# Transposes on TensorE: four 64x64 products with a 64x64 identity in place of one 128x128 transpose

## What is computed

```python
# HGRN2, for each of 8 heads: k * exp(...) and v with positions on the partitions
u_chunk = jnp.einsum('bhnlk,bhnlv->bhnkv', k * jnp.exp(cum_last - cum), v)
# gated MLP, for each of 8 groups: v with positions on the partitions
sv = jnp.einsum('gts,bnsgc->bntgc', w, v) + b_s.T[None, None, :, :, None]
# retention, for each of 4 pairs of heads and 2 layers: keys and values
kv = jnp.einsum('bnjhd,bnjhe,hj->nbhde', kc, vc, zeta)
# attention, for each of 8 heads and 2 layers: the probabilities
o = jnp.einsum('bnhgqs,bnshd->bnqhgd', p.astype(v.dtype), vb)
```

## Time and profile before

| what | value |
|---|---|
| runs, median (lowest to highest) | 2947.54 us (2946.81 to 2949.56) |
| profiled execution, from its first to its last instruction (span) | 2947.4 us |
| TensorE products busy | 2914.6 us, 99% |
| GpSimd busy | 1474.3 us, 50% |
| VectorE busy | 1289.6 us, 44% |
| ScalarE busy | 1093.7 us, 37% |
| mean granted clock of TensorE | 0.998 of full speed |

### The profile page before, as it was taken

The page is one execution under the profiler, slowest core; times in us unless marked ns, Lnnn a source line. Parts: engine busy times, 40 slices in busy tenths (PEclk is TensorE's granted clock), DMA queues, the critical chain, the costliest instruction groups (busy, mean ns, idle before and its releaser), DMA issues.

```text
span 2947.4 us, 52217 instructions
## 1 busy us (share of the span) xinstructions
PE 2914.6 (99%) x20726; PEld 2340.7 (79%) x20726; DVE 1289.6 (44%) x1814; ACT 1093.7 (37%) x1536; POOL 1474.3 (50%) x1824
## 2 busy tenths in 40 slices
PE   9999999999999999999999999999999999999999
PEld 5887778878888777777778888887777777888887
DVE  5827742381111658433657222225944365732210
ACT  4455653352222443224553322224322445432322
POOL 4643345545555556224337555665622433755555
PEclk9999999999999999999999999999999999999999
DMA  7731132313233233226343222333322633432233
GB/s 265 277 102 51 51 99 87 99 52 107 94 99 106 86 109 125 70 75 222 101 160 116 95 94 99 103 105 117 119 71 81 212 110 129 142 99 94 98 101 127
DMA packets 104761, 335.21 MB, mean 114 GB/s; under 512 B 10608, under 2 KB 11024, under 8 KB 103824
## 3 DMA queue, kind: packets, MB, share of 16 engines
q1 hardware_dynamic: 77648, 277.06, 28.6%
q10 hardware_dynamic: 26944, 55.67, 5.1%
HBM read 303.84 MB, written 28.84 MB: 113 GB/s over the span
## 4 chain that ended last, share of the span: by engine, by line
PE 79%; issue 8%; POOL 6%; DVE 4%; ACT 1%; DVEq 1%; DMA 1%; ACTq 0%; POOLq 0%; SPq 0%
PE psum L405 68%; POOL w_lo L376 6%; PE psum L795 5%; DVEq L1720 1%; DMA arena<-scratch 1%; DVE XL L1723 1%; PE psum L1046 0%; PE psum L1026 0%; PE psum L534 0%; PE psum L1040 0%; PE psum L544 0%; PE psum L1062 0%; DVE arena L1741 0%; PE psum L734 0%; PE psum L982 0%
## 5 line engine op out<-in xcount | busy, mean ns | idle before, releaser
L376 POOL TENSOR_TENSOR w_lo<-w_raw,w_hi 128x256 fp32r<-128x256 f32 x1820 | 1474.1, 841 | 1468.4 <-ACT w_hi L1098 1320.1
L405 PE MATMUL psum<-XH,w_hi 128*128 128x512 f32 x2592 | 1047.1, 404 | 10.7 <-DVE arena L1969 3.5
L405 PE MATMUL psum<-XL,w_hi 128*128 128x512 f32 x2592 | 1012.5, 391 | 0.0
L405 PE MATMUL psum<-XH,w_lo 128*128 128x512 f32 x2592 | 1012.4, 391 | 0.0
L1098 ACT ACTIVATE w_hi<-w_raw 128x1024 fp32r<-128x1024 f32 x436 | 460.4, 1056 | 685.0 <-PE psum L405 580.6
L405 PEld LDWEIGHTS psum<-XH,w_hi 128*128 128x128 f32 x2592 | 487.4, 188 | 135.9 <-issue 19.4
L405 PEld LDWEIGHTS psum<-XL,w_hi 128*128 128x128 f32 x2592 | 487.5, 188 | 104.2
L405 PEld LDWEIGHTS psum<-XH,w_lo 128*128 128x128 f32 x2592 | 487.9, 188 | 101.2 <-issue 7.7
L405 PE MATMUL psum<-HH,w_hi 128*128 128x512 f32 x976 | 383.0, 392 | 3.4 <-DVE arena L2354 3.4
L405 PE MATMUL psum<-HL,w_hi 128*128 128x512 f32 x976 | 379.9, 389 | 0.0
L405 PE MATMUL psum<-HH,w_lo 128*128 128x512 f32 x976 | 379.8, 389 | 0.0
(11 more groups left out here) (345 smaller groups left out, 2368.0 us busy)
## 6 DMA issues: line engine op xcount, KB each, us to landing
w_raw<-in_fills SPq DMA_DIRECT2D x456, 512.0 KB, 3.3
scratch<-arena ACTq DMA_DIRECT2D x86, 256.0 KB, 2.1
arena<-in_fills SPq DMA_DIRECT2D x32, 512.0 KB, 4.2
arena<-scratch ACTq DMA_DIRECT2D x10, 1024.0 KB, 7.7
arena<-in_w_ada SPq DMA_DIRECT2D x4, 2048.0 KB, 19.6
H<-scratch ACTq DMA_DIRECT2D x4, 2048.0 KB, 11.5
scratch<-H SPq DMA_DIRECT2D x2, 2048.0 KB, 8.1
arena<-scratch SPq DMA_DIRECT2D x32, 128.0 KB, 3.8
```

The costliest lines, as they stand in the source:

```text
L376: ins = nc.gpsimd.tensor_tensor(w_lo[:, to:to + FILL // 4], w_raw[:, of:of + FILL // 4], w_hi[:, to:to + FILL // 4].bitcast(F32), ALU.subt ...
L405: ins = mm(out_ap, wt[:, w:w + 128], xt[:, x0:x0 + T], start=first and k == 0 and o == 0, stop=last and k == n - 1 and o == 2)
```

## The change

A new helper, `quarter_transposes`, issues four products of 64x64 for each block of 128x128: for each half `j` of the block's columns and each half `i` of its rows, the quarter of the source is the weight and `eye64` is the moving operand. The upper rows go into one bank, the lower rows into a second one. The helper replaces `transposes` at HGRN, gated MLP and retention and the loop of transposes of the attention probabilities. ScalarE's copies keep their size and read the two banks alternately in runs of 64 columns (`turned`, `blocks_of`). In the gated MLP the transposes now need banks 4 and 5, and the products that follow go to banks 6 and 7 in place of 5 and 7.

```diff
+        def turned(b, b1, at, n):
+            both = psum[:, 512 * b:512 * (2 * b1 - b)].rearrange("p (i x) -> p i x", i=2)[:, :, at:at + 64 * n]
+            return both.rearrange("p i (k c) -> p k i c", c=64)
+
+        def blocks_of(ap):
+            return ap.rearrange("p (k i c) -> p k i c", i=2, c=64)
...
+            def quarter_transposes(b, b1, at, src, n=4):
+                for k in range(n):
+                    for j in range(2):
+                        for i, bb in enumerate((b, b1)):
+                            r = slice(64 * i, 64 * i + 64)
+                            ins = mm(bank(bb, 64, at + 64 * k)[64 * j:64 * j + 64], src(k)[r, 64 * j:64 * j + 64], C("eye64", 64)[r],
+                                     start=True, stop=True)
+                return ins
...
-                transposes(4, lambda k: hg("kdec", 128, 128 * k))
-                transposes(5, lambda k: A(60, 128, h * T + 128 * k)).then_inc(sem("hg_tr"), 1)
+                quarter_transposes(4, 5, 0, lambda k: hg("kdec", 128, 128 * k))
+                quarter_transposes(4, 5, 256, lambda k: A(60, 128, h * T + 128 * k)).then_inc(sem("hg_tr"), 1)
...
-                transposes(4, lambda k: A(60, 128, g * T + 128 * k)).then_inc(sem("gm_tr"), 1)
+                quarter_transposes(4, 5, 0, lambda k: A(60, 128, g * T + 128 * k)).then_inc(sem("gm_tr"), 1)
...
-                    ins = mm(bank(5 + 2 * (g % 2), 128, 128 * b), A(42, 128, 128 * b), A(32, 128, 128 * g), start=True, stop=True)
+                    ins = mm(bank(6 + g % 2, 128, 128 * b), A(42, 128, 128 * b), A(32, 128, 128 * g), start=True, stop=True)
...
-                    transposes(2, lambda k: rt("kz", 128, 128 * k))
-                    transposes(3, lambda k: A(RV, 128, T * p + 128 * k)).then_inc(sem("rt_tr"), 1)
+                    quarter_transposes(2, 3, 0, lambda k: rt("kz", 128, 128 * k))
+                    quarter_transposes(2, 3, 256, lambda k: A(RV, 128, T * p + 128 * k)).then_inc(sem("rt_tr"), 1)
...
-                        for s in range(1, 8):
-                            ins = nc.tensor.transpose(bank(4 + 2 * hh, 128, 128 * s), sc(hh, 128, 128 * s), C("ident", 128))
-                        ins.then_inc(sem("at_pt"), 1)
+                        quarter_transposes(4 + 2 * hh, 5 + 2 * hh, 0, lambda k: sc(hh, 128, 128 * (k + 1)), 7).then_inc(sem("at_pt"), 1)
...
-                fn(hg("kdec_t", T), bank(4), ACT.Copy)
-                fn(hg("val_t", T), bank(5), ACT.Copy).then_inc(sem("hg_tm"), 1)
+                fn(blocks_of(hg("kdec_t", T)), turned(4, 5, 0, 4), ACT.Copy)
+                fn(blocks_of(hg("val_t", T)), turned(4, 5, 256, 4), ACT.Copy).then_inc(sem("hg_tm"), 1)
```

More of the change, by code:

```diff
@@ L1360, in _ @@
                 act.wait_ge(sem("gm_tr"), g + 1)
-                fn(A(42), bank(4), ACT.Copy).then_inc(sem("gm_vt"), 1)
+                fn(blocks_of(A(42)), turned(4, 5, 0, 4), ACT.Copy).then_inc(sem("gm_vt"), 1)
                 if g < 6:
@@ L1638, in attend @@
                     act.wait_ge(sem("rt_tr"), n + 1)
-                    fn(rt("kz_t", T), bank(2), ACT.Copy)
-                    fn(rt("v_t", T), bank(3), ACT.Copy).then_inc(sem("rt_tm"), 1)
+                    fn(blocks_of(rt("kz_t", T)), turned(2, 3, 0, 4), ACT.Copy)
+                    fn(blocks_of(rt("v_t", T)), turned(2, 3, 256, 4), ACT.Copy).then_inc(sem("rt_tm"), 1)
                     takes(ATT[p][0])
@@ L1654, in attend @@
                         act.wait_ge(sem("at_pt"), 2 * n + hh + 1)
-                        fn(at("sc", 896, 1024 * hh + 128), bank(4 + 2 * hh, 896, 128), ACT.Copy).then_inc(sem("at_ptc"), 1)
+                        fn(blocks_of(at("sc", 896, 1024 * hh + 128)), turned(4 + 2 * hh, 5 + 2 * hh, 0, 7), ACT.Copy).then_inc(sem("at_ptc"), 1)
                         takes(ATT[p][3 + hh])
@@ L2044, in _ @@
                 dve.wait_ge(sem("gm_sv"), g + 1)
-                tt(chunks(A(40), 128), chunks(bank(5 + 2 * (g % 2)), 128), bc(A(36, 128, g * 128), 4), ALU.add)
+                tt(chunks(A(40), 128), chunks(bank(6 + g % 2), 128), bc(A(36, 128, g * 128), 4), ALU.add)
                 drain()
```

## The result

The changed kernel takes 2958.98 us (median of 5 runs, 2958.02 to 2960.65), the kernel before 2949.56 us (5 runs beside it, 2946.81 to 2950.58). The ratio is 1.0030, with a 95% interval of 1.0018 to 1.0042: slower by 9.4 us, where the forecast was 15.4. The forecast time, 2963.0 us, is only 4 us too high because its base was 2 us too low, and the measured one lies just outside the range of 2959 to 2968.

A forecast was written before the change was run, and what follows sets the result against it. TensorE was taken as the bound; bursts added +6.7 (HGRN, retention), +3.0 (gated MLP) and +6.5 us (probabilities), less 0.8 hidden in waits, so +15.4 us and 2963.0 us, range 2959 to 2968 us (88%).

The forecast's parts named there:

- base: Whole kernel: the profiled execution, 2947.4 us, to which the sum was added, taken as 0.1 us below the runs' median.
- What bounds the kernel: Whole kernel: TensorE is the bound, its products busy for 2914.6 of 2947.4 us.
- The price of the bursts: HGRN, retention, gated MLP, probabilities: quarter bursts cost +0.42, +0.42, +0.37, +0.41 us each over transposes, together +16.2 us.
- neighbours in one column half: Rival, quarter bursts: products writing the same 64 partitions don't overlap, a block takes 0.235 us, +32 us, 2995 us; 5%.
- one pass in place of two: Rival, quarter bursts: a product takes a single record, four cost 0.059 us, 2947 us, no change; 3%.
- transposes that are cheaper than they look: Rival, removed transposes: they give back only half of 0.105 us, sum 14.3 us higher, 2977 us; 1%.
- I leave these waits as they are: Waits for the probabilities, 1.3 and 4.9 us: put at no change, since both sides move together behind the retention burst.
- TensorE pays one for one wherever it doesn't wait: Whole kernel: a change on TensorE is paid one for one wherever it doesn't wait for another engine.
- "absorbed" rival: Rival: TensorE's load waits and some at the chain's other engines absorb half the sum, 2952 to 2957 us; 3%.
- the stretches between the bursts [stay] as they were: Between changed bursts: stretches keep their length while TensorE's busy time rises by about 15 us.
- costs at nothing: ScalarE's two-bank copies, the gated MLP's bank change, 816 more instructions and the waits for probabilities: no added time.

The follow-up runs named there:

- order_crossed: Changed kernel with the quarters of a block in the order (0,0), (64,64), (0,64), (64,0): 2959.91 us.
- before_again: The kernel before, unchanged, run and profiled once more for its granted clock: 2951.75 us (11 runs).
- filled pairs: The kernel before and the changed kernel, both with idle products in five TensorE waits, on two chips: 12.2 and 11.5 us apart.
- before_filled_b: The kernel before with idle products in five TensorE waits, repeated on another chip: 2947.04 us, the kernel before there 2950.01 us.
- after_filled_b: The changed kernel with idle products in the same five waits, repeated on another chip: 2958.50 us, the kernel before there 2950.01 us.
- before_filled: The kernel before with idle products in five TensorE waits of 1.4 to 3.3 us: 2946.58 us, ratio 0.9979 to the kernel before.
- after_filled: The changed kernel with idle products in the same five waits (2 instead of 3 in the HGRN heads): 2958.74 us.
- after_again: The changed kernel, unchanged, run and profiled once more: 2959.58 us (11 runs), +8.1 us against the kernel before.
- second_block_only: The kernel before with the change in retention and attention alone: 2958.56 us, +5.7 us against the kernel before.

## Why the prediction was wrong in size

- **What bounds the kernel** held: TensorE pays for the change.
- **The price of the bursts** held to 0.02 us for all but the first heads' probabilities. With it the rivals of neighbours in one column half (order_crossed) and of one pass in place of two (two records for each product) fell, and the burst prices before and after, taken at the same places, leave no room for transposes that are cheaper than they look. HGRN and retention measured +6.6 us (forecast +6.7), the gated MLP +3.0 (+3.0). The probabilities fell short: second heads +0.40 each, first heads +0.19 each where 0.31 was forecast, together +4.7 in place of +5.7 us. In the first heads the wait ahead of the burst shrank, from 1.3 to 0.4 us for all eight, which the forecast had put at nothing ("I leave these waits as they are"). Sum of the bursts 14.3 us.
- **"TensorE pays one for one wherever it doesn't wait"** was right, but I read the waits only at the bursts. The two HGRN waits for line 1969, 3.5 us in total, were in PE's wait list and in no step of my sum; they took 0.8 us. They stand behind the bursts of their head, and since they shrank by the whole 0.4 us, what ends them doesn't start behind the transposes. The "absorbed" rival had this mechanism with 3% and the wrong places.
- **The step that failed** is "the stretches between the bursts [stay] as they were", and in it the silent one that TensorE has the same clock before and after. I took prices at full clock from single bursts and added them to a profiled execution with 10.2 us at half clock in it, though the mean clock of 0.998 stood in my table. What the half clock costs can be read from the kernel before and before_again, where one has a stretch of it and the other has not: the same products take 1.4 us longer across 3.4 us of half clock (at 330 us) and 2.8 us longer across 6.8 us (at 413 us). For the profiled pair the account then closes: 14.3 us of bursts, less 0.8 us in the HGRN waits, less 1.4 + 2.8 us of half clock that only the kernel before had, make 9.3 us; from the first to the last product of the large matrices the two are 9.2 us apart. The medians agree: with most of the half clock gone the change costs 12.2 and 11.5 us (filled pairs), with the half clock as it falls 8.1 to 9.4 us. The filled medians are 1 to 2 us below 14.3 - 0.8 = 13.5 us. The profiles from the first to the last large product are not (15.1 and 14.1 us), so the rest is likely to lie in the start: before_filled_b reached its first large product 3.4 us later than after_filled_b, behind the half clock shown above, and 4 of 11 runs of before_filled, but 7 of 11 of after_filled, show a mean clock of 1.000. Which of the unprofiled runs had it is not on record.
- **The base.** I took the profiled execution's time as 0.1 us below the median. In every later run the time lies 1.8 us above its span, so that execution took about 2949.2 us. Its kernel's median is 2949.5 to 2952.9 us by chip, so the base was some 2 us low. That error hid 2 us of the miss.
- **Two of the costs at nothing** held: the copies with two banks last 0.60 us (0.598 for line 1639 before) and 0.92 us, and more instructions to fetch left one new wait, of 0.3 us (0.6 in two later profiles).

Why the changed kernel meets less half clock is shown in part. The bursts cut the two HGRN waits from 1.75 to 1.35 us, and behind these half clock fell from 5 of 8 cases to none of 10. Idle products in the same waits give the kernel before 1.6 us and the changed one 0.5, which fits but is within a run's spread. The difference behind the wait of 3.26 us in the first two profiles is chance: before_again has none there and after_again has. That second_block_only gained clock with its HGRN waits at 1.75 us is not explained.

## What to carry to other kernels

Four quarter products are no cheaper than one full-array transpose when both are float32: 0.1175 against 0.105 us here, and each visit to the quarters costs 0.36 us besides. Put small products into quarters where a burst is long or already there, not in short bursts between full-array products. Before adding up microseconds, look for half clock in the stretches of the profile: behind waits of some two microseconds it can hide or fake a quarter to a third of a change this small. Idle products in those waits remove most of it and make a fairer pair to compare, but look at what they cost themselves and at the waits that they leave.

## What the runs showed of the hardware

- A wait of TensorE of 1.75 to 3.3 us is followed by a stretch at 1.2 GHz in some executions and not in others, with the same wait: 3.26 us before 414 us had it in one profile of the kernel before and not in the next. Behind the ten HGRN waits of 1.35 us no profile shows it. Products of 512 columns then start 0.43 us apart. The Trainium skill ("TensorE: Matmul & The Clock Gate", Why this matters for your kernels) warns of idle gaps between bursts of products for this reason. By that rule, the trace agrees, though not in every execution, and also behind waits as short as 1.75 us.
- Idle products of 0.5 us in these waits made the kernel before 6.3 us faster on one chip (ratio 0.9970 to 0.9988) and 3.0 us on another (0.9980 to 0.9998). No other version here is clearly faster than the kernel before.
- A float32 transpose costs half of a plain float32 product with the identity (0.455 against 0.895 us for four), and products in all four quarters cost the same in either order of the quarters.
